# Two state copies of a chunked recurrence shared between ScalarE and VectorE

## The chip, the cores and the metric

The kernel runs on one core of one Trainium2 chip. The metric is the device time of one execution in microseconds (us); of several runs the median counts. The engines are TensorE (PE in the profile, its weight loads PEld), VectorE (DVE), ScalarE (ACT), GpSimd (POOL) and SyncE (SP), which issues most of the DMAs.

## What is computed

A hybrid block (two layers, each with a pooling, a retention and an RWKV-7 branch) is followed by an attention block and a mixture of 32 experts, on 512 tokens of width 1024, in float32. The change lies in the RWKV-7 branch, 8 heads of width 64, whose recurrence over tokens is:

```python
def step(S, inp):
    r_t, w_t, k_t, v_t, a_t, b_t = inp
    sa = jnp.einsum('bhvk,bhk->bhv', S, a_t)
    S = (S * w_t[:, :, None, :] + sa[..., None] * b_t[:, :, None, :]
         + v_t[..., None] * k_t[:, :, None, :])
    return S, jnp.einsum('bhvk,bhk->bhv', S, r_t)
_, y = lax.scan(step, jnp.zeros((B, H, N, N), jnp.float32), xs)
```

## The kernel before, in words

**Chunks.** The kernel replaces the scan over 512 tokens by 8 chunk steps of 64 tokens (`STEPS`), in each of the two layers. All products within a chunk are small matrix products, and only the state (`memory`, 128 x 256) is passed from one step to the next. The heads are kept in two kinds, even (e = 0) and odd (e = 1), one kind on each half of the 128 partitions; every product of a step exists once for each kind, with four heads (`CW`) in it, and has a PSUM bank of its own.

**One step m on TensorE** (`layer_tensor`), in program order:

- w: the product of the chunk's gram matrix with the values (L889), and with the state of the step before (L875, `state_part`, which waits for `s_ready`). It fills the banks w0 and w1, both at its end.
- the gram matrices for the step after the next two (L842, `gram`), in steps 0 to 4.
- u: the inverse of the chunk's triangle times w (L904), first u0, then u1, which the trace shows as eight matmul records each.
- the state's part of the output y (L875 again), from step 1 on.
- a wait for both u copies (`u_ready`), then the update of the state (L917, in steps 0 to 6) and the rest of y (L921).

**The copies out of PSUM.** Each product has to be copied to SBUF before TensorE can use it. ACT copies w0 and w1 (L1143) and then y0 and y1 (L1148). DVE takes, in this order: the mask on one gram bank (L1343, `gram_mask(m + 3, 0)`), u0 and u1 (L1353), the addition to the state (L1359; a copy, L1357, in step 0), its decay (L1360, which reads two tensors in SBUF, `memory` and `e_end`, and gives `s_ready`), and the mask on the other gram bank (L1343, `gram_mask(m + 3, 1)`). Each engine works its list off in order.

**Banks.** A table `jobs`, written in the order in which TensorE opens banks, says for each product which semaphore tells that its bank has been drained. The eight banks are used in turn, so TensorE opens a bank only when the job eight places earlier has been drained (`open_bank`). A step has nine jobs: w0, w1, gram 0, gram 1, u0, u1, s, y0, y1. The first gram job of a step thus waits for the second gram mask of the step before.

**Weight chunks meanwhile.** The projections use weights in chunks of 512 KB. SP loads a chunk once TensorE has used the one it replaces; ACT rounds it (L1041, `high`), POOL subtracts the rounded part to get the rest (L1525, `low`, 128 x 1024, both inputs in SBUF). The projections of retention that follow the chunk steps use chunks of which the first three are rounded within the steps, one in each of the steps 1, 3 and 5:

```python
if m % 2 == 1 and m // 2 < RING:
    high(FIRST["retq"] + m // 2)
```

POOL follows with `low` for that chunk, then copies values for a later even step (L1592). After the steps TensorE goes on to `project_tok("retq", ...)`, DVE to the head norm of y.

Of the kernel before, what the change touches and what calls it, by code (L numbers as in the profile page):

```python
# [21 lines left out]
CW = W // P  # L22
# [131 lines left out]
def program(nc, ada, wstream, lparams, gparams, consts, distances, experts, last_norm, x_in, pos_in, out):  # L154
    with ExitStack() as ctx:
# [22 lines left out]
        def inc(ins, name, by=1):  # L178
            given[name] = given.get(name, 0) + by
            ins.then_inc(SEM[name], by)  # L180
# [128 lines left out]
        def job(name, drained, k):  # L309
            jobs.append((name, drained, k))  # L310
# [43 lines left out]
                    job(f"{name}{x}{e}", ready, 1 + 2 * x + e)  # L354
        for m in range(STEPS):
            for e in range(2):
                job(f"w{m}{e}", "w_ready", 1 + 2 * m + e)
            if m + GRAMS_FIRST < STEPS:
                gram_jobs(m + GRAMS_FIRST)
            for e in range(2):  # L360
                job(f"u{m}{e}", "u_ready", 1 + 2 * m + e)
            if m < STEPS - 1:
                job(f"s{m}", "s_added", 1 + m)
            for e in range(2):
                job(f"y{m}{e}", "y_ready", 1 + 2 * m + e)
# [68 lines left out]
        for name, per in (("bank_full", NJ), ("params_loaded", 16), ("x_done", 8), ("adaload0", 16 * ADA_B // 2), ("adaload1", 16 * ADA_B // 2),  # L434
                          ("ada_step", KD * ADA_B), ("mods_step", 4), ("omm_ready", 2), ("xsq_ready", 8), ("xsq_summed", 7),
                          ("rms_ready", 1), ("rms_sqrt", 1),
                          ("h_scaled", 8), ("h_ready", 8), ("mix_scaled", 13), ("mixed", 13), ("wl_tanh", 1),
                          ("g_ready", 4), ("a_ready", 4), ("kk_ready", 2), ("ka_ready", 4), ("kss_sqrt", 1),
                          ("k_mod", 1), ("rk_ready", 1), ("kk_unit", 3), ("kn_stored", 16), ("kn_spread", 32), ("bonus_ready", 4),
                          ("pu_ready", 4), ("pg_ready", 4), ("pool_step", 2 + 4 + 10 + 4 * 3), ("pool_d", 4),  # L440
                          ("pool_done", 4), ("g_sum", 1), ("g_prev", 1), ("exp_prev", 1), ("exp_plus", 1),
                          ("exp_minus", 1), ("ar_ready", 2), ("bk_ready", 2), ("tok_ready", 5 * NT),
                          ("x_kept", 16), ("x_back", 16), ("dg_ready", 2), ("corner_ready", 2), ("dg_stored", 8 * NT * SUBS), ("dg_gathered", 16),
                          ("inv_step", 2 * SUB - 1), ("inv_ready", 2), ("inv_stored", 32), ("inv_spread", 16 * (SUBS + 2)), ("z_clear", 1),
                          ("gram_ready", 2 * STEPS), ("p_ready", 4), ("z_ready", 4), ("v_copied", NT),
                          ("w_ready", 2 * STEPS), ("u_ready", 2 * STEPS), ("y_ready", 2 * STEPS),
                          ("s_added", STEPS - 1), ("s_ready", STEPS - 1), ("y_norm", 7), ("y_sqrt", 1), ("y_scaled", 4),
                          ("rwkv_done", 4), ("rg_ready", 4), ("ret_tok", 12), ("retg_ready", 4),
                          ("rot_step", 6), ("rot_ready", 2), ("qT_ready", 4), ("qd_ready", 4), ("kT_ready", 4),
                          ("ktail_ready", 1), ("pret_ready", 4), ("o_ready", 4), ("R_ready", 3), ("o_norm", 7),  # L450
                          ("o_sqrt", 1), ("ret_done", 4), ("gate_sig", 24), ("merged", 40),
                          ("w_high", LAYER_B - len(WHOLE)), ("w_split", LAYER_B - len(WHOLE)), ("quarter_used", 9), ("h_high", 8),
                          ("br_high", 3), ("br_split", 3), ("m_high", 8), ("m_split", 8)):
            sem(name, per, layer_ctx)
            LAYER_SEMS.append(name)
# [232 lines left out]
        def layer_tensor(pe, L):  # L688
            state_ = {"job": 0}

            def after(name, k=None):
                pe.wait_ge(SEM[name], L * PER[name] + (PER[name] if k is None else k))
# [187 lines left out]
            for m in range(STEPS):  # L880
                uv, bk = per_head(uv_of(m)), per_head(bk_of(m))

                after("gram_ready", 2 * m + 2)
                if m % 2 == 0:
                    after("v_copied", m // 2 + 1)
                o_w = [open_bank(f"w{m}{e}") for e in range(2)]
                for e in range(2):
                    for c in range(CW):
                        mm = nc.tensor.matmul(o_w[e][u_side(m), heads[c]], gm[:, m % 4, e, c, 1, :], uv[:, e, c, :],  # L889
                                              start=(c == 0), stop=(m == 0 and c == CW - 1), skip_group_check=True)  # L890
                    if m == 0:
                        full(mm)
                if m > 0:
                    after("s_ready", m)
                    state_part(o_w, KK, m, u_side(m), False, True)
                if m + GRAMS_FIRST < STEPS:
                    gram(m + GRAMS_FIRST)

                for e in range(2):
                    o_u = open_bank(f"u{m}{e}")  # L900
                    after("w_ready", 2 * m + e + 1)
                    after("z_ready", 2 * (m // 4) + 2)
                    for c in range(CW):
                        mm = nc.tensor.matmul(o_u[u_side(m), heads[c]], zt[u_side(m), RW_H * (m // 2) + 2 * c + e, :],  # L904
                                              w_sb[u_side(m), e * CW * RW_D + c * RW_D:e * CW * RW_D + (c + 1) * RW_D], start=True, stop=True)
                    full(mm)

                if m < STEPS - 1:
                    o_s = open_bank(f"s{m}")
                o_y = [open_bank(f"y{m}{e}") for e in range(2)]  # L910
                if m > 0:
                    state_part(o_y, R_, m, v_side(m), True, False)
                after("u_ready", 2 * m + 2)
                if m < STEPS - 1:
                    for c in range(CW):
                        for e in range(2):
                            mm = nc.tensor.matmul(o_s[side_of[e], heads[c]], bk[:, e, c, :], uv[:, e, c, :], start=True, stop=True)  # L917
                    full(mm)
                for e in range(2):
                    for c in range(CW):  # L920
                        mm = nc.tensor.matmul(o_y[e][v_side(m), heads[c]], gm[:, m % 4, e, c, 0, :], uv[:, e, c, :],  # L921
                                              start=(m == 0 and c == 0), stop=(c == CW - 1), skip_group_check=True)
                    full(mm)
# [97 lines left out]
        def layer_scalar(act, L):  # L1021
# [117 lines left out]
                        o = bank(f"{name}{x}{e}")[at, :].rearrange("p (i t) -> p i t", t=SUB)  # L1139
                        inc(nc.scalar.activation(dst(at, slice(2 * RW_H * x, 2 * RW_H * (x + 1))), o, ACT.Copy), ready)  # L1140
            for m in range(STEPS):
                for e in range(2):
                    inc(nc.scalar.activation(w_sb[u_side(m), e * CW * RW_D:(e + 1) * CW * RW_D], bank(f"w{m}{e}")[u_side(m), 0:CW * RW_D], ACT.Copy), "w_ready")  # L1143
                if m % 2 == 1 and m // 2 < RING:
                    high(FIRST["retq"] + m // 2)
                for e in range(2):
                    o = bank(f"y{m}{e}")[v_side(m), 0:CW * RW_D].rearrange("p (c f) -> p c f", c=CW)
                    inc(nc.scalar.activation(per_head(y_tok[v_side(m), m // 2, :])[:, e], o, ACT.Copy), "y_ready")  # L1148
# [66 lines left out]
        def layer_vector(dve, L):  # L1215
# [129 lines left out]
            for m in range(GRAMS_FIRST):  # L1345
                for e in range(2):
                    gram_mask(m, e)
            for m in range(STEPS):
                if m + GRAMS_FIRST < STEPS:
                    gram_mask(m + GRAMS_FIRST, 0)  # L1350
                for e in range(2):
                    o = bank(f"u{m}{e}")[u_side(m), 0:CW * RW_D].rearrange("p (c f) -> p c f", c=CW)
                    inc(v.tensor_copy(per_head(uv_of(m)[u_side(m)])[:, e], o), "u_ready")  # L1353
                if m < STEPS - 1:
                    o = bank(f"s{m}")[:, 0:CW * RW_D].rearrange("p (c f) -> p c f", c=CW)
                    if m == 0:
                        step(v.tensor_copy(memory, o), "s_added")  # L1357
                    else:
                        step(v.tensor_tensor(memory, o, memory, ALU.add), "s_added")  # L1359
                    inc(v.tensor_tensor(memory, memory, e_end[:, :, m:m + 1].broadcast_to([P, CW, RW_D]), ALU.mult), "s_ready")  # L1360
                    after("s_ready", m + 1)
                if m + GRAMS_FIRST < STEPS:
                    gram_mask(m + GRAMS_FIRST, 1)
# [1587 lines left out]
```

## Time and profile before

| What | Value |
|---|---|
| Median of three runs | 1835.14 us (1833.32 to 1837.72) |
| The profiled execution's own time | 1840.28 us |
| Its span | 1838.2 us |
| Mean granted TensorE clock in it | 0.968 of 2.4 GHz |
| PE busy | 1718.2 us (93%) |
| DVE busy | 1036.0 us (56%) |
| ACT busy | 800.7 us (44%) |
| POOL busy | 632.0 us (34%) |
| Chunk steps, first layer | from about 252 to 300 us in the span |
| Chunk steps, second layer | from about 844 to 892 us in the span |

Times within the profile are counted from the start of the span. A row of the timeline gives the start, the duration, the engine, the line, what is written and read, and in brackets how long the engine had been idle and what ended the wait. Rows of one kind that touch are merged (x2 is two instructions, whose duration is from the first's start to the last's end). The busy shares are averages over the whole program; what a copy in the chunk steps costs is read from the steps.

### The profile page before, as it was taken

The page shows a single profiled execution, that of the slowest core. Times are in us where ns is not written, and L with a number is a line of the kernel's source. Part 1 is how long each engine was busy: PE and PEld are TensorE (multiplying, and loading weights), DVE is VectorE, ACT ScalarE, POOL GpSimd, SP SyncE. Part 2 cuts the span into 40 slices and gives each one's busy share as a digit, 9 for nine tenths or more (in the row PEclk, how much of TensorE's full clock was granted, in tenths as well). Part 3 has the DMA queues.
Part 4 walks back from the last instruction along what each step waited for, and adds up shares of the span by engine and source line. Part 5 has one row for each costly group of instructions (what it writes and reads, how often), then busy time and mean ns, then how long its engine had stood idle before and what let it go on. Part 6 is the DMA issues. An engine that isn't in the chain of part 4 may idle for free. (4 is left out here: it accounts for less than half of the span.)

```text
span 1838.2 us, 26011 instructions
## 1 busy us (share of the span) xinstructions
PE 1718.2 (93%) x10688; PEld 1373.8 (75%) x10688; DVE 1036.0 (56%) x1367; ACT 800.7 (44%) x1200; POOL 632.0 (34%) x344
## 2 busy tenths in 40 slices
PE   8999989999999899899999999989999999987783
PEld 6877778888888787688888888868888986544441
DVE  4346744666665325584556766443116627866675
ACT  2455522333223335542333222344337736866673
POOL 1336612424444434751243444433421021322210
PEclk7999989999999899998999999989999999999997
DMA  8223321215444323322122544333420067999994
GB/s 344 81 92 106 90 77 36 92 58 192 171 166 171 126 92 96 96 85 77 54 85 66 209 175 169 138 126 126 149 92 1 1 240 265 382 388 395 389 392 178
DMA packets 82605, 287.97 MB, mean 157 GB/s; under 512 B 30473, under 2 KB 30601, under 8 KB 65332
## 3 DMA queue, kind: packets, MB, share of 16 engines
q1 hardware_dynamic: 76708, 275.87, 41.6%
q0 software_dynamic: 5040, 8.25, 1.4%
q8 instruction: 88, 1.44, 0.3%
q10 hardware_dynamic: 736, 2.14, 0.3%
q14 instruction: 33, 0.27, 0.0%
HBM read 274.50 MB, written 22.61 MB: 162 GB/s over the span
## 5 line engine op out<-in xcount | busy, mean ns | idle before, releaser
L1525 POOL TENSOR_TENSOR wmem_r<-wmem,wmem_r 128x1024 fp32r<-128x1024 f32 x170 | 420.2, 2473 | 696.4 <-ACT wmem_r L1041 685.5
L721 PE MATMUL banks<-h_hi_r,wmem_r 128*128 128x512 f32 x1632 | 511.2, 392 | 6.9 <-POOL wmem_r L1525 6.9
L721 PEld LDWEIGHTS banks<-h_hi_r,wmem_r 128*128 128x128 f32 x1632 | 307.9, 189 | 77.0 <-POOL wmem_r L1525 9.4
L1041 ACT ACTIVATE wmem_r<-wmem 128x1024 fp32r<-128x1024 f32 x170 | 180.2, 1060 | 405.2 <-DMA wmem<-wstream 402.2
L721 PE MATMUL banks<-hT_r,wmem_r 128*128 128x512 f32 x816 | 319.0, 391 | 0.0
L721 PEld LDWEIGHTS banks<-hT_r,wmem_r 128*128 128x128 f32 x816 | 154.0, 189 | 31.3
L2725 DVE TENSOR_TENSOR slots_r<-slots,wmem_r 128x1024 fp32r<-128x1024 f32 x102 | 121.9, 1217 | 57.7 <-ACT wmem_r L2418 52.1
L2806 POOL TENSOR_TENSOR wmem_r<-wmem,wmem_r 128x1024 fp32r<-128x1024 f32 x30 | 74.8, 2493 | 202.3 <-ACT wmem_r L2276 202.3
L992 PE MATMUL banks<-slots_r,wmem_r 128*128 128x512 f32 x512 | 127.7, 389 | 0.0
L1465 DVE SCALAR_TENSOR_TENSOR ztp<-xT,c_act,ztp 128x256 f32<-128x256 f32 x168 | 122.8, 731 | 6.0
L741 PE MATMUL banks<-wmem_r,h_hi_r 128*128 128x512 f32 x384 | 118.9, 391 | 0.0
L2418 ACT ACTIVATE wmem_r<-slots 128x1024 fp32r<-128x1024 f32 x102 | 102.1, 1052 | 37.6 <-DMA slots<-experts 36.3
L992 PEld LDWEIGHTS banks<-slots_r,wmem_r 128*128 128x128 f32 x512 | 96.1, 188 | 20.0
L2212 PE MATMUL banks<-wmem_r,gm_mem_r 128*128 128x512 f32 x248 | 104.9, 423 | 0.0
L1827 POOL DMA_INDIRECT y_tok_dram<-ztp,y_idx x32 | 32.3, 1008 | 200.4 <-PE banks L1799 119.9
L1812 PE MATMUL banks<-slots,gm_mem 128*64 128x512 f32 x216 | 55.4, 633 | 29.9 <-issue 29.9
L741 PEld LDWEIGHTS banks<-wmem_r,h_hi_r 128*128 128x128 f32 x384 | 71.6, 188 | 14.8
L2212 PE MATMUL banks<-slots_r,gm_mem_r 128*128 128x512 f32 x204 | 80.8, 396 | 0.0
L1262 DVE SCALAR_TENSOR_TENSOR slots<-banks,lpar,slots 128x511 f32<-128x511 f32 x24 | 18.0, 749 | 101.4 <-ACT slots L1064 74.8
L741 PE MATMUL banks<-wmem_r,hT_r 128*128 128x512 f32 x192 | 74.8, 389 | 0.0
L1962 PE MATMUL banks<-h_hi_r,wmem_r 128*128 128x512 f32 x240 | 74.6, 390 | 0.0
L2212 PEld LDWEIGHTS banks<-wmem_r,gm_mem_r 128*128 128x128 f32 x248 | 46.9, 189 | 37.0 <-issue 22.7
(450 smaller groups left out, 3043.1 us busy)
## 6 DMA issues: line engine op xcount, KB each, us to landing
wmem<-wstream SPq DMA_DIRECT2D x206, 512.0 KB, 3.3
slots<-experts SPq DMA_DIRECT2D x80, 1024.0 KB, 24.5
xT<-ada SPq DMA_DIRECT2D x24, 1024.0 KB, 5.8
xT<-experts SPq DMA_DIRECT2D x16, 1024.0 KB, 25.0
slots<-ada SPq DMA_DIRECT2D x8, 1024.0 KB, 18.0
x_keep<-xT SPq DMA_DIRECT2D x2, 2048.0 KB, 17.4
xT<-x_keep SPq DMA_DIRECT2D x2, 2048.0 KB, 8.1
dil_rows<-dil_once SPq DMA_DIRECT2D x1, 2560.0 KB
```

The lines of the kernel that those rows point to most:

```text
L721: mm = nc.tensor.matmul(o, r(lhs[:, k, :]), r(rhs[:, k, :]), start=(k == 0 and i == 0), stop=(k == KD - 1 and i == 2))
L741: mm = nc.tensor.matmul(o[n], r(lhs[:, 2 * b + k, n * P:n * P + P]), r(rhs[:, k, :]), start=(b == 0 and k == 0 and i == 0), stop=(b == CW ...
L992: mm = nc.tensor.matmul(o, r(lhs[:, i % 2 * CW + k, :]), r(rhs[:, k, :]), start=(k == 0 and j == 0), stop=(k == CW - 1 and j == 2))
L1041: inc(nc.scalar.activation(r(chunk(b)[0]), w, ACT.Copy), "w_high")
L1465: step(v.scalar_tensor_tensor(acc, w_k, c_k, acc, ALU.mult, ALU.add), "ada_step")
L1525: inc(g.tensor_tensor(r(lo), lo, r(hi), ALU.subtract), "w_split")
L1812: mm = nc.tensor.matmul(bank[side[i], :], h_t[:, f * SLOT:(f + 1) * SLOT], w[:, f, halves[i]], start=(f == 0), stop=(f == 1))
L1962: mm = nc.tensor.matmul(o, r(lhs[:, k, :]), r(rhs[:, k, :]), start=(k == 0 and i == 0), stop=(k == KD - 1 and i == 2))
L2212: mm = nc.tensor.matmul(banks[0:2 * SLOT, 2 + e % 2], r(both), r(w[i][:, kk, :]), start=(half == 0 and kk == 0 and i == 0), stop=(half == ...
L2418: nc.scalar.activation(r(raw_hi[g % NHI][:, cols]), raw[j % NRAW][:, cols], ACT.Copy).then_inc(SEM["eh_ready"], 1)
L2725: v.tensor_tensor(r(lo), lo, r(raw_hi[g % NHI][:, cols]), ALU.subtract).then_inc(SEM["el_ready"], 1)
L2806: nc.gpsimd.tensor_tensor(r(lo), lo, r(hi), ALU.subtract).then_inc(SEM["a_split"], 1)
```

## The change

Each of w and u is now shared between the two engines, one kind of heads each. ACT copies w0 and u1, DVE copies w1 and u0. The counters `w_ready` and `u_ready` are split into one for each kind. On ACT the u1 copy stands behind w0 and ahead of the rounding of the weight chunk; on DVE the w1 copy stands ahead of the first gram mask of the step. TensorE's order is the same; it waits for both u counters where it waited for one.

```diff
@@ table of jobs
-                job(f"w{m}{e}", "w_ready", 1 + 2 * m + e)
+                job(f"w{m}{e}", f"w_ready{e}", 1 + m)
-                job(f"u{m}{e}", "u_ready", 1 + 2 * m + e)
+                job(f"u{m}{e}", f"u_ready{e}", 1 + m)
@@ semaphores
-                          ("w_ready", 2 * STEPS), ("u_ready", 2 * STEPS), ("y_ready", 2 * STEPS),
+                          ("w_ready0", STEPS), ("w_ready1", STEPS), ("u_ready0", STEPS), ("u_ready1", STEPS), ("y_ready", 2 * STEPS),
@@ layer_tensor
                 for e in range(2):
                     o_u = open_bank(f"u{m}{e}")
-                    after("w_ready", 2 * m + e + 1)
+                    after(f"w_ready{e}", m + 1)
...
-                after("u_ready", 2 * m + 2)
+                after("u_ready0", m + 1)
+                after("u_ready1", m + 1)
@@ ScalarE
             for m in range(STEPS):
-                for e in range(2):
-                    inc(nc.scalar.activation(w_sb[u_side(m), e * CW * RW_D:(e + 1) * CW * RW_D], bank(f"w{m}{e}")[u_side(m), 0:CW * RW_D], ACT.Copy), "w_ready")
+                inc(nc.scalar.activation(w_sb[u_side(m), 0:CW * RW_D], bank(f"w{m}0")[u_side(m), 0:CW * RW_D], ACT.Copy), "w_ready0")
+                o = bank(f"u{m}1")[u_side(m), 0:CW * RW_D].rearrange("p (c f) -> p c f", c=CW)
+                inc(nc.scalar.activation(per_head(uv_of(m)[u_side(m)])[:, 1], o, ACT.Copy), "u_ready1")
                 if m % 2 == 1 and m // 2 < RING:
                     high(FIRST["retq"] + m // 2)
@@ VectorE
             for m in range(STEPS):
+                inc(v.tensor_copy(w_sb[u_side(m), CW * RW_D:2 * CW * RW_D], bank(f"w{m}1")[u_side(m), 0:CW * RW_D]), "w_ready1")
                 if m + GRAMS_FIRST < STEPS:
                     gram_mask(m + GRAMS_FIRST, 0)
-                for e in range(2):
-                    o = bank(f"u{m}{e}")[u_side(m), 0:CW * RW_D].rearrange("p (c f) -> p c f", c=CW)
-                    inc(v.tensor_copy(per_head(uv_of(m)[u_side(m)])[:, e], o), "u_ready")
+                o = bank(f"u{m}0")[u_side(m), 0:CW * RW_D].rearrange("p (c f) -> p c f", c=CW)
+                inc(v.tensor_copy(per_head(uv_of(m)[u_side(m)])[:, 0], o), "u_ready0")
```

How the order on ACT changes in steps 0, 1 and 2. Before (the first row is w0 and w1 of step 0, `slots` with x2 is y, `wmem_r` is the rounding of a weight chunk):

```order
L1143 ACTIVATE wu_sb<-banks 64x256 x2
L1148 ACTIVATE slots<-banks 64x4x64 x2
L1143 ACTIVATE wu_sb<-banks 64x256 x2
L1041 ACTIVATE wmem_r<-wmem 128x1024
L1148 ACTIVATE slots<-banks 64x4x64 x2
L1143 ACTIVATE wu_sb<-banks 64x256 x2
L1148 ACTIVATE slots<-banks 64x4x64 x2
```

And now, with the u1 copy in L1145 (it writes `rstd`, `slots` or `wu_sb`, depending on the step):

```order
L1143 ACTIVATE wu_sb<-banks 64x256
L1145 ACTIVATE rstd<-banks 64x4x64
L1150 ACTIVATE slots<-banks 64x4x64 x2
L1143 ACTIVATE wu_sb<-banks 64x256
L1145 ACTIVATE slots<-banks 64x4x64
L1042 ACTIVATE wmem_r<-wmem 128x1024
L1150 ACTIVATE slots<-banks 64x4x64 x2
```

In step 1 the rounding, L1041 and now L1042, followed the copies of w; it now follows the copy of u1.

On DVE, step 1, with what each instruction waits for. Before:

```order
L1343 TENSOR_TENSOR gm_mem<-banks,cst 128x512 [waits bank_full]
L1353 COPY slots<-banks 64x4x64 [waits bank_full] x2
L1359 TENSOR_TENSOR state<-banks,state 128x256 [waits bank_full]
L1360 TENSOR_TENSOR state<-state,e_end 128x256 [waits s_added]
L1343 TENSOR_TENSOR gm_mem<-banks,cst 128x512 [waits bank_full,s_ready]
```

And now:

```order
L1351 COPY wu_sb<-banks 64x256 [waits bank_full]
L1345 TENSOR_TENSOR gm_mem<-banks,cst 128x512 [waits bank_full]
L1355 COPY slots<-banks 64x4x64 [waits bank_full]
L1361 TENSOR_TENSOR state<-banks,state 128x256 [waits bank_full]
L1362 TENSOR_TENSOR state<-state,e_end 128x256 [waits s_added]
L1345 TENSOR_TENSOR gm_mem<-banks,cst 128x512 [waits bank_full,s_ready]
```

The w1 copy (L1351) has come in ahead of the first mask, and one of the two u copies is gone; the state's addition and decay and the second mask keep their places. The lists of TensorE and POOL are as before.

## Rows read from the trace of the kernel before

**Rows 1.** Busy time by windows: first layer's steps, us, then PE, PEld, DVE, ACT, POOL, clock
```profile
252.00:300.00 48.00, 43.73 (x905) 41.52 (x902) 20.28 (x40) 15.49 (x38) 8.56 (x5) 0.90 0.01 3
```

**Rows 2.** Timeline (start, duration, us): wait of step 0, then step 2, first layer
```profile
258.75 1.12 PE L917 MATMUL banks<-rstd,slots 128*64 128x64 f32 x16 [0.61 <-DVE rstd L1353]
...
269.73 0.69 DVE L1343 TENSOR_TENSOR gm_mem<-banks,cst 128x512 f32<-128x512 f32 x1 [1.49 <-PE banks L842]
...
270.33 0.22 PE L904 MATMUL banks<-wu_sb,ztp 64*64 64x64 f32 x1
...
270.46 0.77 DVE L1353 COPY wu_sb<-banks 64x256 f32<-64x256 f32 x2
...
271.28 0.28 PE L917 MATMUL banks<-wu_sb,slots 128*64 128x64 f32 x2 [0.44 <-DVE wu_sb L1353]
```

**Rows 3.** Timeline: step 1 and the start of step 2, first layer
```profile
263.49 0.37 ACT L1143 ACTIVATE wu_sb<-banks 64x256 f32<-64x256 f32 x1
263.76 1.05 ACT L1041 ACTIVATE wmem_r<-wmem 128x1024 fp32r<-128x1024 f32 x1
...
264.76 0.22 PE L904 MATMUL banks<-wu_sb,ztp 64*64 64x64 f32 x1
...
264.88 2.35 POOL L1525 TENSOR_TENSOR wmem_r<-wmem,wmem_r 128x1024 fp32r<-128x1024 f32 x1 [29.71 <-ACT wmem_r L1041]
...
265.58 0.69 PE L917 MATMUL banks<-slots 128*64 128x64 f32 x16 [0.30 <-DVE slots L1353]
...
266.77 0.75 DVE L1360 TENSOR_TENSOR state<-state,e_end 128x256 f32<-128x256 f32 x1
...
267.55 0.69 DVE L1343 TENSOR_TENSOR gm_mem<-banks,cst 128x512 f32<-128x512 f32 x1
...
268.06 0.62 PE L875 MATMUL banks<-state,slots 64*64 64x64 f32 x13
...
268.46 0.32 PE L842 MATMUL banks<-slots 64*64 64x128 f32 x1
```

**Rows 4.** Timeline: step 5 and step 6, first layer
```profile
287.10 0.22 PE L904 MATMUL banks<-wu_sb,ztp 64*64 64x64 f32 x1
...
287.39 2.36 POOL L1525 TENSOR_TENSOR wmem_r<-wmem,wmem_r 128x1024 fp32r<-128x1024 f32 x1 [8.15 <-ACT wmem_r L1041]
...
289.01 1.02 DVE L1360 TENSOR_TENSOR state<-state,e_end 128x256 f32<-128x256 f32 x1
...
290.31 0.68 PE L875 MATMUL banks<-state,slots 64*64 64x64 f32 x16
...
291.02 0.38 ACT L1143 ACTIVATE wu_sb<-banks 64x256 f32<-64x256 f32 x1 [1.16 <-PE banks L875]
...
291.50 0.94 PE L904 MATMUL banks<-wu_sb,ztp 64*64 64x64 f32 x13 [0.51 <-ACT wu_sb L1143]
...
292.39 0.22 PE L904 MATMUL banks<-wu_sb,ztp 64*64 64x64 f32 x1
...
293.13 0.69 PE L917 MATMUL banks<-wu_sb,slots 128*64 128x64 f32 x16 [0.23 <-DVE wu_sb L1353]
```

**Rows 5.** Source L1360, the state's decay: count, ns min/median/max, first and last start
```profile
L1360 DVE TENSOR_TENSOR state<-state,e_end x14: 424/426/1018, 260.4 to 884.3; 128x256 f32<-128x256 f32 x14
```

**Rows 6.** Another two-input DVE operation: timeline beside POOL's subtraction, and source L1465
```profile
539.17 2.40 POOL L1525 TENSOR_TENSOR wmem_r<-wmem,wmem_r 128x1024 fp32r<-128x1024 f32 x1 [3.07 <-ACT wmem_r L1041]
539.36 2.50 DVE L1465 SCALAR_TENSOR_TENSOR ztp<-xT,c_act,ztp 128x256 f32<-128x256 f32 x1
L1465 DVE SCALAR_TENSOR_TENSOR ztp<-xT,c_act,ztp x168: 483/485/2727, 437.2 to 1156.3; 128x256 f32<-128x256 f32 x168
```

**Rows 7.** Windows of three stretches, columns as in rows 1: clock after idle TensorE
```profile
148.80:150.90 2.10, 0.01 (x1) 0.00 (x0) 2.10 (x1) 1.53 (x3) 2.10 (x2) 1.00 0.53 156
152.40:155.80 3.40, 3.40 (x10) 2.63 (x9) 3.40 (x5) 2.01 (x2) 3.32 (x3) 0.50 0.00 0
774.30:775.60 1.30, 0.08 (x5) 0.06 (x1) 1.30 (x3) 1.28 (x3) 1.30 (x1) 1.00 0.00 0
```

## The prediction

> **What bounds the kernel now.** I read the stretch of the chunk steps by windows first: in the 48 us of one layer TensorE is busy for 43.73, DVE for 20.28 and ACT for 15.49, at a mean clock of 0.90 [rows 1]. So TensorE is what fills the steps, and ACT and DVE cost only where one of their copies ends later than TensorE's other work. The timeline of single steps says where. In step 2 the last matmul of u1 ends at 270.33 + 0.22 = 270.55, DVE is busy with a gram mask until 269.73 + 0.69 = 270.42, copies u0 and then u1 from 270.46 to 271.23, and TensorE begins L917 at 271.28, after an idle 0.44 us [rows 2]. The pattern is alike in all steps, and in both layers. Step 0 waits 0.61 [rows 2], step 1 0.30 [rows 3], step 6 0.23 [rows 4]. The w copies cost little. In steps 0 to 4 the gram matmuls lie over them, and in steps 5 to 7 TensorE waits for the copy of w0, which stays on ACT (L904 starts 0.10 us after the end of that copy, 291.02 + 0.38 = 291.40 to 291.50) [rows 4]; the second w copy ends some 0.3 us later, and TensorE needs it only after eight more matmuls.
>
> Next I looked at what else runs in these steps. In step 1 ACT rounds a weight chunk (L1041) straight after its w copies, from 263.76 to 264.81, and POOL subtracts from 264.88 to 267.23 (L1525). DVE's state update L1360, asked for at 266.77, takes 0.75 us [rows 3], where the median of its fourteen is 0.426 [rows 5]. In step 5 POOL's instruction ends at 287.39 + 2.36 = 289.75, and L1360, from 289.01, takes 1.02 and ends at 290.03 [rows 4]. Each time L1360 ends 0.28 or 0.29 us after POOL's instruction. That is the number to see in these rows: nothing of the update gets done while POOL's subtraction runs. At present this costs nothing, since TensorE starts the state matmuls of the next step (L875) only at 268.06, 0.54 us after L1360's end at 267.52 [rows 3].
>
> **The change, part by part.**
>
> *w1 to DVE.* ACT loses a copy of 0.38 and DVE gains one of about 0.4 (its two u copies of step 2 take 0.77 together) [rows 2, 4]. DVE is idle when w1 is full, and the gram mask behind the new copy has to wait for TensorE's gram matmuls anyway: in step 2 DVE starts that mask at 269.73, as those end [rows 2]. w0 is not copied sooner. I take 0.
>
> *u1 to ACT.* u0 stays behind the gram mask on DVE and ends at about 270.9 in step 2, well before u1 can. u1 can be copied by ACT as soon as it is full: 0.03 us to start (L875 ends at 290.99, ACT starts at 291.02), 0.38 of copy, 0.07 to 0.10 until TensorE runs [rows 4], together 0.50 us after the last u matmul. Today the distance is 271.28 - 270.55 = 0.73 in step 2 [rows 2], 265.58 - 264.98 = 0.60 in step 1 [rows 3] and 293.13 - 292.61 = 0.52 in step 6 [rows 4]. Gains: 0.23 in steps 2 and 4, 0.10 in steps 0, 1 and 3, 0.02 in steps 5 to 7. That is 0.46 + 0.30 + 0.06 = 0.82 us a layer, 1.6 us in two, between 0.5 (if ACT takes its highest latency, and each wait 0.03 more) and 2.5 (if TensorE waited for nothing but u0).
>
> *The rounding L1041 is moved past u1.* In steps 1, 3 and 5 ACT rounded the chunk between w and y. Now u1 stands ahead of it, and u1 is full 1.1 us after the w copies end. In step 1: u1 is full at 264.98, copied from 265.01 to 265.39; L1041 starts 0.10 before that end, as it now does behind w1 (263.76 against 263.49 + 0.37) [rows 3], so from 265.29 to 266.34; POOL 0.08 later, from 266.42 to 268.77. L1360 comes up at 266.77 less the 0.10 gained, so at 266.67, 0.25 us behind POOL. Today POOL has only 0.46 us left at that moment; then it has 2.10. L1360 ends at 268.77 + 0.29 = 269.06, TensorE can start L875 at 269.11 instead of 268.06: 1.05 us late. Behind L1360 on DVE stands a gram mask, which moves from 267.55 to 269.09, ends at 269.78, and frees the bank that the next gram matmuls (L842) need, since they open the bank used eight jobs earlier. They start, 0.06 after it, at 269.84 instead of 268.46 [rows 3]: 1.38 us late, in which the 1.05 is contained. Step 3 is the same. In step 5 u1 is full at 287.10 + 0.22 = 287.32, copied until 287.73; the rounding runs 287.63 to 288.68, POOL 288.76 to 291.12, L1360 ends at 291.41, and L875 starts at 291.46 instead of 290.31 [rows 4]: 1.15 us; no gram follows it. A layer loses 1.38 + 1.38 + 1.15 = 3.91 us, in which the gains of these three steps are already taken off. Two more things move with the rounding, and I cost them at nothing: ACT's y copies behind it (it ends at 266.34, and y0 is full only after the 0.69 us of L917 from 265.48 and eight matmuls more, so later than that), and POOL's copy for the values of a step two or three steps on (L1592).
>
> That the wait is for the whole instruction is shown outside the steps too: POOL's subtraction from 539.17 to 541.57, and a DVE operation with two SBUF inputs asked for at 539.36 that takes 2.50 and ends at 541.86, again 0.29 after; the median of that operation is 0.485 [rows 6]. The Trainium skill (SBUF — State Buffer, "SBUF: two separate sides") says that a DVE operation with two SBUF inputs and a GpSimd operation lock out one another for a whole instruction, whichever starts first; by that rule each of the six stalls is as worked out, and the trace agrees, with 2.50 against 0.485 us. By a rule of shared bandwidth, which that section rejects, the change would be a small gain (rival B).
>
> *The sum.* A layer: -0.10 (step 0) - 0.23 - 0.23 (steps 2 and 4) - 0.04 (steps 6 and 7) + 3.91 = +3.31 us; two layers +6.6. Bounds: 2 x (3 x 1.05 - 0.60) = +5.1 if the gram matmuls don't wait besides, 2 x 3.91 = +7.8 if the gains in the other steps fail. All that follows in a layer stands behind TensorE (the projections of retention, then the merge), weight chunks are loaded as TensorE frees them, and the experts' first loads wait for the attention, so I see nothing that takes the delay up. The profiled execution took 1840.28 us (span 1838.2), 5.1 above the median of 1835.14; on the median the forecast is 1835.1 + 6.6 = 1841.7, 0.36% slower. What a measurement of this kernel can tell from no change is about 0.2%, 3.7 us.
>
> **The rivals.**
>
> *B: DVE is not locked out.* If L1360 came up ahead of POOL, or were let in between, it would be done well before L875 needs it, with 0.54 us in hand today. Only the gain of 0.82 us a layer is then left: 1835.1 - 1.6 = 1833.5, 0.09% faster, within what is called the same. If the two shared the reads, step 1 gives the rate: 0.14 us of work in 0.46 us beside POOL, so 1.4 us for the whole update, which ends at 268.07 and holds L875 up by 0.15; six of these give 0.9 us back, 1834.4. Against both: the 2.50 us at 539.36 [rows 6], and the 0.28 to 0.29 us in steps as unlike as 1 and 5. For the first: POOL leads by a mere 0.25 us. That is the point from which it decides: if POOL starts over 0.25 us later than I work out, or L1360 as much sooner, the stall is gone.
>
> *C: the delay is caught up later.* If one layer's stall were made good, because something after the steps waits for a transfer or for POOL anyway, 3.3 us are left: 1838.4. For it: some 550 us of program follow each layer's steps, and I have not followed every wait in them. Against: the chunks that are loaded there are loaded as TensorE frees them.
>
> *D: the stalls cost clock.* TensorE stands still for 1.05 to 1.4 us in six places. After an idle 2.1 us at 148.8 the granted clock fell to 0.50 from 152.4 to 155.8; after an idle 1.3 at 774.3 it stayed at 1.00 [rows 7]. Those 3.4 us at 1.2 GHz in place of 2.4 GHz cost 1.7 us; at all six places 10 us more: 1851.9. The Trainium skill (TensorE: Matmul & The Clock Gate, HAM oscillation) tells of a kernel that fell back to half clock in every wait between its bursts. The nearer row is the one of 1.3 us, so I give this little.
>
> **How the numbers follow.** The forecast has 0.75, B 0.12, C 0.08, D 0.05. The forecast's own range is 1838.5 to 1844.5 (the bound of +5.1 below and about half the way to +7.8 above, and some 1.5 us of scatter of medians: the three runs shown lie within 4.4 us). The range to hold the time 8 times in 10 takes in C and part of the way to B: 1835.0 to 1846.0; B and D stay outside, 0.17. Slower by over 0.2% (above 1838.8): nearly all of the forecast, D, and a third of C, 0.79; within 0.2%: most of B and the rest of C, 0.19; faster 0.02.
>
> **What would show it.** In the profile after: L1360 (now L1362) at 2.3 to 2.4 us six times instead of 0.75 and 1.02; POOL's subtractions starting at 1.5 us (steps 1 and 3) and 1.4 us (step 5) later in their step, ahead of it; L875 with an idle of about 1.1 us that DVE's state update ends, and L842 waiting 0.3 us more after steps 1 and 3; steps 2 and 4 shorter by 0.23 in the wait ahead of L918. The prediction is wrong if the L1362s stay under 1.1 us, or if the steps become longer by 3.3 us a layer and the total doesn't.

## The result, and the profile after

The changed kernel took 1846.17 us in the median of six runs (1843.0 to 1849.78), the kernel before 1836.33 us (1833.32 to 1841.89): a ratio of 1.0057, with a 95% interval of 1.0041 to 1.0072, so 7.5 to 13 us slower. Measured once more beside other kernels it was 1.0066 (1.0051 to 1.008). The prediction had the side, and the mechanism of the stalls, at +6.6 us; the median lies 0.17 us above the upper end of its range. That it lies just outside is in part scatter: the six runs of the kernel before have a median 1.2 us above that of the three shown in the table, and as a difference the two medians are 9.8 us apart. What the forecast lacks is not scatter, as the steps show below.

The page after, its first lines (share of the span, instructions), and the granted clock in 40 slices:

```profile
span 1842.7 us, 26025 instructions
...
PE 1714.5 (93%) x10688; PEld 1368.8 (74%) x10688; DVE 1050.0 (57%) x1367; ACT 802.3 (44%) x1200; POOL 638.8 (35%) x344
...
PEclk7999989999999999998999999999999999999997
```

DVE is busy 14 us longer and PE about as long as before; nothing on this page tells where 10 us went. The profiled execution took 1844.69 us, 4.4 more than that of before, because the half clock outside the steps falls differently in each execution (the stretch of 0.50 that ends in step 0 was over 5.3 us earlier here, at 256.3 and not 261.6; outside steps 1 to 7 the trace has 107 us at 0.50 here and 121 us before). So I compare the steps, and take the whole from the medians.

Step 1 and the start of step 2 in the first layer after (timeline as in rows 3):

```profile
262.91 0.22 PE L904 MATMUL banks<-wu_sb,ztp 64*64 64x64 f32 x1
...
262.93 0.41 DVE L1355 COPY slots<-banks 64x256 f32<-64x256 f32 x1
263.17 0.38 ACT L1145 ACTIVATE slots<-banks 64x256 f32<-64x256 f32 x1 [1.43 <-PE banks L904]
263.45 1.04 ACT L1042 ACTIVATE wmem_r<-wmem 128x1024 fp32r<-128x1024 f32 x1
263.69 0.69 PE L918 MATMUL banks<-slots 128*64 128x64 f32 x16 [0.27 <-ACT slots L1145]
...
264.57 2.35 POOL L1527 TENSOR_TENSOR wmem_r<-wmem,wmem_r 128x1024 fp32r<-128x1024 f32 x1 [28.79 <-ACT wmem_r L1042]
264.87 2.33 DVE L1362 TENSOR_TENSOR state<-state,e_end 128x256 f32<-128x256 f32 x1
...
267.23 0.69 DVE L1345 TENSOR_TENSOR gm_mem<-banks,cst 128x512 f32<-128x512 f32 x1
267.25 0.68 PE L875 MATMUL banks<-state,slots 64*64 64x64 f32 x16 [1.01 <-DVE state L1362]
...
267.98 1.10 PE L842 MATMUL banks<-slots 64*64 64x128 f32 x32
```

POOL starts 0.30 us ahead of the state's decay (0.25 was worked out), ends at 266.92, and the decay ends 0.28 us later, at 267.20, after 2.33 us instead of the 0.75 of [rows 3]. TensorE stands idle for 1.01 us ahead of L875, and L842, which took 0.40 us to follow L875 in [rows 3], takes 0.73, because the gram mask ends only at 267.92. From the start of L918 to that of L842 it is 267.98 - 263.69 = 4.29 us here, and from L917 to L842 before 268.46 - 265.58 = 2.88 us [rows 3].

Steps 5 and 6 after, same columns:

```profile
289.12 2.35 POOL L1527 TENSOR_TENSOR wmem_r<-wmem,wmem_r 128x1024 fp32r<-128x1024 f32 x1 [9.09 <-ACT wmem_r L1042]
289.42 2.33 DVE L1362 TENSOR_TENSOR state<-state,e_end 128x256 f32<-128x256 f32 x1
...
289.69 1.10 PE L889 MATMUL banks<-wu_sb,gm_mem 128*64 128x64 f32 x16
291.81 0.68 PE L875 MATMUL banks<-state,slots 64*64 64x64 f32 x16 [1.01 <-DVE state L1362]
...
293.00 0.94 PE L904 MATMUL banks<-wu_sb,ztp 64*64 64x64 f32 x13 [0.51 <-issue]
...
294.77 1.12 PE L918 MATMUL banks<-wu_sb,slots 128*64 128x64 f32 x16
295.64 1.84 PE L922 MATMUL banks<-wu_sb,gm_mem 128*64 128x64 f32 x16
...
297.33 0.34 PE L889 MATMUL banks<-slots,gm_mem 128*64 128x64 f32 x3
```

Windows of the changed kernel in both layers (columns as in rows 1), and of the kernel before at the same place:

```profile
294.00:297.20 3.20, 3.17 (x47) 3.02 (x45) 0.95 (x3) 0.76 (x2) 0.00 (x0) 0.50 0.03 5
888.00:891.10 3.10, 3.10 (x39) 3.10 (x39) 0.85 (x2) 0.76 (x2) 0.00 (x0) 0.50 0.00 0
```

```profile
288.00:291.00 3.00, 2.99 (x64) 2.78 (x62) 1.44 (x2) 0.76 (x2) 1.75 (x1) 1.00 0.02 5
883.00:886.00 3.00, 2.91 (x62) 2.84 (x64) 0.88 (x3) 0.75 (x2) 0.00 (x0) 1.00 0.00 0
```

This is the part that the forecast lacks: a stretch at 0.50 of the clock, in both layers, late in step 6. L918 takes 1.12 us there instead of 0.69, and the sixteen matmuls of L922 take 1.84 instead of 1.10. Step 6 lasts 297.33 - 289.69 = 7.64 us; before it was 5.30 (from 289.28 to 294.58; its middle is in [rows 4]).

### The profile page after: what moved, and what is told of

Its sections match the earlier page's. It is cut to its first block and busy times, and to the rows that moved or that the text cites. A ratio compares the mean times of both kernels' runs of the same rounds, so it can differ in the third digit from the quotient of the medians.

```text
span 1842.7 us, 26025 instructions
## 1 busy us (share of the span) xinstructions
PE 1714.5 (93%) x10688; PEld 1368.8 (74%) x10688; DVE 1050.0 (57%) x1367; ACT 802.3 (44%) x1200; POOL 638.8 (35%) x344
## 5 line engine op out<-in xcount | busy, mean ns | idle before, releaser
L1042 ACT ACTIVATE wmem_r<-wmem 128x1024 fp32r<-128x1024 f32 x170 | 180.1, 1060 | 404.7 <-DMA wmem<-wstream 401.5
L1467 DVE SCALAR_TENSOR_TENSOR ztp<-xT,c_act,ztp 128x256 f32<-128x256 f32 x168 | 129.0, 768 | 6.0
```

The lines of the kernel that those rows point to most:

```text
L1042: inc(nc.scalar.activation(r(chunk(b)[0]), w, ACT.Copy), "w_high")
L1467: step(v.scalar_tensor_tensor(acc, w_k, c_k, acc, ALU.mult, ALU.add), "ada_step")
```

## The experiments

For each run I give two numbers against the kernel before. The first is the measured ratio of the runs, in us of 1836. The second is the time of steps 1 to 7 (from the first matmul of L889 in step 1 to the first of the projection behind step 7), both layers together, read from the trace. It leaves step 0 out, in which the clock differs from one execution to the next. Before, these steps took 38.16 and 38.01 us. In the first layer before and of rounding first, and in the second of stall filled, the half clock of step 0 reaches into step 1 and adds 0.14 to 0.24 us, so the last column is good to some 0.2 us.

| Kernel | Ratio (95% interval) | In us | Steps 1 to 7, both layers | Against before |
|---|---|---|---|---|
| the change | 1.0057 (1.0041 to 1.0072) | +10.5 | 42.64 + 42.90 | +9.4 |
| the change again | 1.0066 (1.0051 to 1.008) | +12.1 | 42.64 + 42.82 | +9.3 |
| rounding first | 0.9995 (0.9985 to 1.0004) | -0.9 | 37.85 + 37.62 | -0.7 |
| POOL waits | 0.9998 (0.9986 to 1.001) | -0.4 | 37.61 + 37.61 | -0.9 |
| late rounding only | 1.0045 (1.0032 to 1.0058) | +8.3 | 42.32 + 42.52 | +8.7 |
| stall of step 5 only | 1.0021 (1.001 to 1.0032) | +3.9 | 40.08 + 40.01 | +3.9 |
| stalls of 1 and 3 only | 1.0029 (1.0018 to 1.0041) | +5.3 | 40.31 + 40.30 | +4.4 |
| stall filled | 1.003 (1.0015 to 1.0045) | +5.5 | 41.40 + 41.54 | +6.8 |
| only w shared | 1.0007 (0.9995 to 1.0019) | +1.3 | 38.53 + 38.52 | +0.9 |
| one counter | 0.9993 (0.9982 to 1.0003) | -1.3 | 37.09 + 37.08 | -2.0 |
| two waits | 1.0021 (1.0009 to 1.0034) | +3.9 | 38.53 + 38.64 | +1.0 |

**Rounding first.** The change, with one move undone.

```diff
+                if m % 2 == 1 and m // 2 < RING:
+                    high(FIRST["retq"] + m // 2)
                 o = bank(f"u{m}1")[u_side(m), 0:CW * RW_D].rearrange("p (c f) -> p c f", c=CW)
                 inc(nc.scalar.activation(per_head(uv_of(m)[u_side(m)])[:, 1], o, ACT.Copy), "u_ready1")
-                if m % 2 == 1 and m // 2 < RING:
-                    high(FIRST["retq"] + m // 2)
```

> The change, with the rounding of the weight chunk put back ahead of the u1 copy on ScalarE (w0, rounding, u1, y). If the loss comes from POOL's subtraction getting ahead of the state's decay (theory 1), POOL starts some 1.8 us earlier in steps 1, 3 and 5, the decay takes at most 1 us, TensorE doesn't wait for it, no granted clock of one half appears around step 6, and only the shorter wait for u is left: 1.6 us faster than before (0.1%), that is 10 to 11 us faster than the change. If the loss comes from the copies themselves being on the other engine (rival), it stays at +7 us or more.

The whole loss is gone (0.9995), with both shared copies in place, and no half clock shows in step 6 or 7. The decay's source line:

```profile
L1362 DVE TENSOR_TENSOR state<-state,e_end x14: 424/426/710, 260.2 to 884.2; 128x256 f32<-128x256 f32 x14
```

Its longest is now 0.71 us, in the change it was 2.33. The gain of 1.6 us is not there in full: 0.7 in the steps. What is missing is taken up below (one counter).

**POOL waits.** The change, with POOL's subtraction held back.

```diff
                 if n > 0:
+                    if n <= 3:
+                        after("s_ready", 2 * n)
                     low(FIRST["retq"] + n - 1, FIRST["retq"] + n)
```

> The change as it is, but POOL starts each of the three subtractions within the steps only after the state's decay of the same step (s_ready). Theory 1 (the two operations lock each other out): the decay is back at 0.43 us in all steps, no wait of TensorE for it, 1.6 us faster than before. Rival (the late rounding on ScalarE is what costs, by way of the y copies or the chunk): still slower than before by 5 us or more, since the rounding stays late and the subtraction is later still.

The rounding stays as late as in the change and the subtraction comes later still, and the loss is gone all the same (0.9 us of gain in the steps, where 1.6 was expected; the runs can't tell it from no change). Timeline of step 1 in this run:

```profile
263.91 0.42 DVE L1362 TENSOR_TENSOR state<-state,e_end 128x256 f32<-128x256 f32 x1
...
264.37 0.69 DVE L1345 TENSOR_TENSOR gm_mem<-banks,cst 128x512 f32<-128x512 f32 x1
264.41 2.36 POOL L1527 TENSOR_TENSOR wmem_r<-wmem,wmem_r 128x1024 fp32r<-128x1024 f32 x1 [30.56 <-DVE state L1362]
```

The decay takes 0.42 us, and the mask beside POOL's operation, which reads PSUM and one tensor in SBUF, takes its usual 0.69. So it is the two operations' overlap that costs, not the late rounding.

**Late rounding only.** The kernel before with all its copies, and only the start of the rounding moved.

```diff
                 if m % 2 == 1 and m // 2 < RING:
+                    after("bank_full", FULL[f"u{m}1"])
                     high(FIRST["retq"] + m // 2)
```

> The kernel before, all copies where they were; only the rounding in steps 1, 3, 5 waits until u1 is full, as it does in the change. Theory 1: POOL starts at about 266.1 in step 1 (0.6 us ahead of the decay), the decay takes about 2.0 us, the state matmuls come 0.8 us late and the gram matmuls 1.1 us (steps 2 and 4), step 6 0.9 us late: 3.1 us a layer, +6 us in all, and up to 3 us more if the granted clock falls after step 5 as in the change. Rival (the moved copies cost): no difference from before.

No copy has changed engine, and the kernel is as slow as with the change, but for 2 us (8.7 us in the steps, inside the 6 to 9 that were expected). In its step 1:

```profile
262.76 2.35 POOL L1526 TENSOR_TENSOR wmem_r<-wmem,wmem_r 128x1024 fp32r<-128x1024 f32 x1 [29.65 <-ACT wmem_r L1041]
...
263.38 2.02 DVE L1361 TENSOR_TENSOR state<-state,e_end 128x256 f32<-128x256 f32 x1
...
265.45 0.68 PE L875 MATMUL banks<-state,slots 64*64 64x64 f32 x16 [0.72 <-DVE state L1361]
```

POOL leads by 0.62 here, the decay takes 2.02 (2.0 expected), and it ends at 265.40, again 0.29 us behind POOL's end. The half clock is there too, in both layers (292.3 to 295.7 and 886.2 to 889.6), here after a shorter wait:

```profile
289.87 0.68 PE L875 MATMUL banks<-state,slots 64*64 64x64 f32 x16 [0.80 <-DVE state L1361]
...
292.40:295.60 3.20, 3.02 (x38) 2.91 (x36) 1.08 (x3) 0.43 (x2) 0.00 (x0) 0.50 0.03 5
886.30:889.50 3.20, 3.20 (x40) 3.20 (x38) 0.85 (x2) 0.75 (x2) 0.00 (x0) 0.50 0.00 0
```

This settles that the move of the rounding, alone, is enough for the loss.

**Stall of step 5 only, stalls of steps 1 and 3 only.** The change, with POOL's wait of above under `if n < 3` in the one and `if n == 3` in the other.

> The change, POOL waiting for the state's decay in steps 1 and 3 only; the stall of step 5 stays. Stalls cost by theory 1: 1.15 us a layer, less 0.8 us of gain, so +0.5 us in two layers without a clock effect. If the granted clock falls because of the stall ahead of step 6 alone, half clock still shows from about step 6 on, and the time is +3.5 us against before; if it falls because of the stalls together, full clock stays and the time is +0.5 us.

> The change, POOL waiting for the state's decay in step 5 only; the stalls of steps 1 and 3 stay. By theory 1 the two stalls cost 1.38 us each a layer, less 0.5 us of gains in the other steps: 2.2 us a layer, +4.5 us in all. If the clock falls because of the stall ahead of step 6, it stays at full clock here: +4.5 us. If two stalls are enough for it, half clock shows somewhere after step 4 and the time is +7 us or more.

With the stall of step 5 alone, the half clock comes in both layers, and with the two others alone it does not. Windows of late step 6 in the first, and of steps 5 and 6 in the second:

```profile
290.80:294.00 3.20, 3.00 (x36) 3.03 (x37) 0.85 (x2) 0.60 (x3) 0.00 (x0) 0.50 0.03 5
881.30:884.50 3.20, 3.06 (x41) 2.90 (x38) 0.85 (x2) 0.62 (x2) 0.00 (x0) 0.50 0.00 0
```

```profile
285.30:290.60 5.30, 4.53 (x99) 4.24 (x98) 2.37 (x6) 2.41 (x6) 0.00 (x0) 1.00 0.01 3
290.60:295.90 5.30, 4.53 (x100) 4.25 (x99) 1.66 (x5) 1.50 (x5) 2.34 (x1) 1.00 0.01 3
```

Both times are as the local reading had them: +3.9 where +3.5 was expected, and +5.3 (+4.4 in the steps) for +4.5. The two add up to 3.9 + 4.4 = 8.3 us in the steps; both contain the gain of 0.9 us that POOL waits shows, so together they make 8.3 + 0.9 = 9.2, against 9.4 of the change.

**Stall filled.** The change, with TensorE kept busy in the wait ahead of step 6.

```diff
-                for e in range(2):
+                for e in (0, 1, 0, 1) if m == 6 else (0, 1):
                     for c in range(CW):
                         mm = nc.tensor.matmul(o_w[e][u_side(m), heads[c]], gm[:, m % 4, e, c, 1, :], uv[:, e, c, :],
                                               start=(c == 0), stop=(m == 0 and c == CW - 1), skip_group_check=True)
```

> The change, with the w product of step 6 (16 matmul records) computed twice into the same banks, which fills most of TensorE's wait there with work. Theory 2 (the half clock after step 5 comes from TensorE standing still in that wait): no half clock at step 6, the steps of a layer last about 48.6 us in place of 50.1, and the time is 3 us below the change, so about +7 us against before. If the half clock doesn't come from the idle time, it stays: +10 us, and perhaps more for the added matmuls.

The timeline and the windows of step 6 in this run:

```profile
287.53 2.33 DVE L1362 TENSOR_TENSOR state<-state,e_end 128x256 f32<-128x256 f32 x1
...
287.80 2.03 PE L889 MATMUL banks<-wu_sb,gm_mem 128*64 128x64 f32 x32
289.92 0.68 PE L875 MATMUL banks<-state,slots 64*64 64x64 f32 x16
```

```profile
287.80:294.20 6.40, 5.54 (x116) 5.19 (x115) 3.58 (x5) 1.52 (x5) 1.78 (x1) 1.00 0.01 3
882.50:888.80 6.30, 5.44 (x114) 5.09 (x113) 3.48 (x5) 1.42 (x5) 1.71 (x1) 1.00 0.01 3
```

The decay is as late as in the change, TensorE does 32 matmuls in place of 16, and the clock stays at 1.00. Step 6 takes 6.40 us. So TensorE standing still in that wait is needed for the half clock. Steps 6 and 7 take 6.40 + 4.93 = 11.33 us here, 12.57 and 12.83 in the change: the clock costs 1.2 to 1.5 us a layer. The steps say 2.6 us better than the change. The runs say 6.6 against the change measured again beside it (1.003 against 1.0066, each good to some 2.7 us), so they agree on the side and leave the size open.

**Only w shared.** The change, both u copies on DVE, each with its own counter.

```diff
-                o = bank(f"u{m}1")[u_side(m), 0:CW * RW_D].rearrange("p (c f) -> p c f", c=CW)
-                inc(nc.scalar.activation(per_head(uv_of(m)[u_side(m)])[:, 1], o, ACT.Copy), "u_ready1")
...
                 inc(v.tensor_copy(per_head(uv_of(m)[u_side(m)])[:, 0], o), "u_ready0")
+                o = bank(f"u{m}1")[u_side(m), 0:CW * RW_D].rearrange("p (c f) -> p c f", c=CW)
+                inc(v.tensor_copy(per_head(uv_of(m)[u_side(m)])[:, 1], o), "u_ready1")
```

> Only w is shared (w1 on DVE), both u copies stay on DVE and the rounding follows w0. Theory: nothing waits for w1, so the same as before within 0.5 us; POOL's subtraction starts 0.27 us earlier. If DVE's new copy delays the gram mask and u0, slower by 0.1 to 0.4 us a step, up to +5 us.

The runs can't tell it from before. The trace can: 0.9 us more in the steps, though the masks and the u copies start as before. The end of step 5's u copies, and the next matmul:

```profile
282.06 0.41 DVE L1355 COPY slots<-banks 64x256 f32<-64x256 f32 x1
282.62 0.59 PE L918 MATMUL banks<-slots 128*64 128x64 f32 x13 [0.30 <-DVE slots L1355]
```

It is 282.62 - 282.47 = 0.15 us from the copy to the matmul, where the kernel before has 0.05 (271.23 to 271.28) [rows 2]. The copy is on the same engine. What differs there is that TensorE waits for two counters.

**One counter.** As rounding first, both u copies counting up one semaphore and one wait for it.

```diff
-                job(f"u{m}{e}", f"u_ready{e}", 1 + m)
+                job(f"u{m}{e}", "u_ready", 2 + 2 * m)
...
-                after("u_ready0", m + 1)
-                after("u_ready1", m + 1)
+                after("u_ready", 2 * m + 2)
```

> As the run with the rounding ahead of the u1 copy, but both u copies count up one semaphore again and TensorE waits once for it. There, and with both u copies on DVE too, the first matmul of the state's update came 0.145 us after the last u copy, against 0.056 in the kernel before. If the second wait costs this 0.09 us, it is gone in all sixteen steps: 0.056 again, steps of 5.43, 5.41 and 5.25 us in place of 5.52, 5.50 and 5.34, 1.4 us less in all, 2 to 2.5 us below the kernel before (0.12%). If the 0.09 us comes from something else, the steps stay as they were.

Step 2 in rounding first, then in one counter:

```profile
270.50 0.38 ACT L1147 ACTIVATE wu_sb<-banks 64x256 f32<-64x256 f32 x1 [1.44 <-PE banks L904]
271.02 0.28 PE L918 MATMUL banks<-wu_sb,slots 128*64 128x64 f32 x2 [0.27 <-ACT wu_sb L1147]
```

```profile
267.62 0.38 ACT L1146 ACTIVATE wu_sb<-banks 64x256 f32<-64x256 f32 x1 [1.44 <-PE banks L904]
268.05 0.34 PE L917 MATMUL banks<-wu_sb,slots 128*64 128x64 f32 x4 [0.17 <-ACT wu_sb L1146]
```

From the copy's end it is 0.14 us in the first and 0.05 in the second. Steps 1 to 6 became 5.43 and 5.25 us, close to what was expected, and 2.0 us less in all. (Step 0 keeps its 0.145 us, so the second wait is gone from fourteen steps and not from sixteen.) The measured ratio of 0.9993 (0.9982 to 1.0003) agrees with that but doesn't show it against no change; it is the best of all these kernels by the steps in the trace, and not shown to be faster than the kernel before.

**Two waits.** The kernel before, with a second wait and nothing else.

```diff
+                after("u_ready", 2 * m + 1)
                 after("u_ready", 2 * m + 2)
```

> The kernel before with a second wait of TensorE ahead of the state's update, for a count of the same semaphore that is reached earlier (u0), so that only the wait itself is added. If a second wait costs 0.09 us: the distance from the last u copy to the matmul is 0.145 us in place of 0.056, each step is 0.09 us longer, 1.4 us in all. If it costs only because the counters are two different semaphores, nothing changes.

Step 5, the last u copy (x2 is u0 and u1) and the next matmul:

```profile
285.80 0.88 DVE L1354 COPY slots<-banks 64x256 f32<-64x256 f32 x2 [1.99 <-PE banks L904]
286.82 0.39 PE L918 MATMUL banks<-slots 128*64 128x64 f32 x6 [0.31 <-DVE slots L1354]
```

The distance from the last copy to the matmul is 0.145 us, the steps are as long as in the run with only w shared (5.65, 5.76, 5.38, 5.36), so it is the second wait and not the second semaphore. The runs give +3.9 us (+1.7 to +6.2), more than the 1.0 us seen in the steps of its trace; the rest is open.

**The change again** was run on one chip with stalls of 1 and 3 only, stall filled, and only w shared.

> The change again, beside the others on one chip: +9.8 us against before as first measured, made of 3.4 us a layer of stalls less gains and about 1.5 us a layer of half clock after step 5. If the half clock was an accident of the one profiled execution, this profile shows full clock in steps 6 and 7 of at least one layer.

The same half clock, at the same place in both layers:

```profile
292.60:295.80 3.20, 3.18 (x50) 3.02 (x47) 1.05 (x3) 0.69 (x2) 0.00 (x0) 0.50 0.02 5
886.50:889.80 3.30, 3.08 (x37) 3.11 (x38) 0.85 (x2) 0.70 (x3) 0.00 (x0) 0.50 0.00 0
```

In all profiles the half clock at step 6 is there in each of the eight layers with the unfilled stall of step 5, and in none of the sixteen others, those of the kernel before among them.

## Why the prediction was wrong, point by point

- **Side and mechanism: right.** The rounding moved past u1, POOL came to stand ahead of the state's decay (0.30 us, 0.25 worked out), and the decay waited for the whole of POOL's operation: 2.33 us six times (2.3 to 2.4 forecast). L875 came with an idle of 1.01 us (1.05 to 1.15 forecast as delays), L842 0.33 us later still, as the bank table said. Steps 1 and 2 together lost 1.1 us in the second layer, where the clock was full in both kernels (5.52 + 6.85 against 5.56 + 5.70); the forecast, 1.38 less 0.23, was 1.15. That no copy need change engine for this is shown by late rounding only, and that the rest of the change makes no net loss is shown by POOL waits.
- **Rival B: out.** DVE is held for the whole of POOL's instruction, however long POOL's lead (0.62 us in late rounding only, 0.30 in the change), and the decay ends 0.28 or 0.29 us after POOL in each. It takes 0.42 us alone, so some 0.14 us of it is done by then, after 0.46 us beside POOL in step 1 before and after 2.05 us in the change alike. At the shared rate worked out for this rival the decay would have taken 1.4 us in the change and not 2.33. The Trainium skill (SBUF — State Buffer, "SBUF: two separate sides") calls the pair of ports an exclusive lock that the one who starts first keeps for its whole instruction; the 2.33 and 2.02 us agree with it.
- **Rival D: the step that failed.** The granted clock had a chance of 0.05 and nothing in the sum, on the ground that the nearer row was an idle 1.3 us at 774.3 that did not lower the clock [rows 7]. What the runs showed in its place is a fall to 0.50 after the stall of step 5, in both layers, that costs 2.7 us. That row was the wrong neighbour. I looked at the length of one idle and not at what stands around it. In step 6 the stall of 1.01 us is followed, 0.68 us of matmuls later, by an idle of 0.51 us ahead of L904, with no gram matmuls between; in steps 2 and 4 the gram matmuls follow at once, and there the clock held. Steps 5, 6 and 7 have the 0.51 us in every kernel, and without the stall it never lowered the clock. That the gram matmuls are what held it in steps 2 and 4 is my reading: no run took them away or put them into step 6. The Trainium skill (TensorE: Matmul & The Clock Gate, HAM oscillation) tells of a kernel whose clock falls in the waits between its bursts of work, but its waits are for a DMA and several times as long as the 1.01 and 0.51 us here. Stall filled agrees with it in the side, in that matmuls put into the wait kept the clock at 1.00. The rival's price for one place was near (1.7 us, measured 1.2 and 1.5), its number of places was not: two of six, so 2.7 us and not 10. The true case was the forecast plus this third of rival D. That is 1841.7 + 2.7 = 1844.4, which the range still holds; the 1.2 us by which the median of the kernel before moved, and 0.6 us more, took the median past 1846.0.
- **The gain from sharing u: half its size, and hardly any part of the miss.** The sum had 0.50 us from the last u matmul to the update, from the 0.07 to 0.10 that TensorE takes to follow ACT. It was 263.69 - 263.13 = 0.56, since the second wait adds 0.09. The added wait stood in the diff, and the prediction costed it at nothing. Steps 2 and 4 gained 0.20 to 0.21 instead of 0.23, steps 1 and 3 0.04 instead of 0.10, and steps 5 to 7 lost 0.01 to 0.05 each (0.9 us in POOL waits, where 1.6 was forecast). In steps 1, 3 and 5 this makes no difference to the total of the change: the stall behind them ends at a time that is counted from u1 being full, by way of ACT and POOL, and a smaller gain only makes the stall shorter. Stall filled shows the sum without the clock: the steps lost 6.8 us, where the forecast, less its 0.2 us of gain in step 0, has 6.8. With the 2.7 us of clock that is 9.5 us, against +9.4 in the steps and +10.5 and +12.1 in the runs. What the runs have above the steps, 1 to 3 us, was not traced.
- **w1 to DVE at nothing: right but for its wait.** Only w shared loses 0.9 us in the steps, and its steps are as long as those of two waits, which shares no copy; so the two counters for u account for it.
- **Rival C: nothing was caught up later.** The steps lost 9.4 us and the runs 10.5.

## What to carry to other kernels

When an operation is put ahead of another in an engine's list, follow what the second one triggers on other engines; here a copy of 0.38 us, with the wait for u1 that comes with it, moved a POOL instruction by 1.5 us, ahead of the one DVE instruction of the step that it holds up. Where two engines can share a state's copies, let both count one semaphore, so that the consumer waits once. And when you judge what a stall may do to TensorE's clock, look at the other idle times around it, in the part of the program where TensorE has least to do, and not at its length alone; how far each counts these runs leave open.

## What the runs showed of the hardware

- A second wait of TensorE ahead of a matmul costs 0.09 us, even for a count that was reached some 0.4 us earlier (0.145 us from the copy to the matmul in place of 0.05 to 0.056, in steps 1 to 7 of both layers, in every kernel with two waits). In step 0, where waits for banks stand ahead of the same matmul, it is about 0.145 us in all kernels, the one before among them.
- A DVE operation of two SBUF inputs (0.42 us alone) that comes up behind the start of POOL's subtraction of 2.35 us ends 0.28 to 0.29 us after POOL's end, with leads of POOL from 0.30 to 2.1 us; one that reads PSUM and one SBUF tensor is not held (0.69 us either way).
- The granted clock fell to 0.50 (1.2 GHz) late in step 6 after two idle times of TensorE in that step, of 1.01 us (0.80 in late rounding only) and 0.51 us, in 8 of 8 layers. In the first layer of the change the third idle, behind u, can have no part in it: the clock is at 0.50 from 293.9, and up to 294.7 TensorE is busy. It stayed at 1.00 from step 2 on in all 16 layers in which the wait ahead of step 6 is missing or filled with matmuls, and in the steps 2 and 4 that have a wait of 1.01 us with gram matmuls soon behind it. What exactly the chip counts is not shown by these runs.
